# The modulation map of a diffusion step: from split matmuls through the weight ring to plain float32 on four column groups

## What is computed

```python
mod = (jax.nn.silu(cond) @ P['w_ada'][l] + P['b_ada'][l]).reshape(cond.shape[0], N_MOD, D_MODEL)
shift1, scale1, gate1, shift2, scale2, gate2 = (mod[:, i, None, :] for i in range(N_MOD))
h = rmsnorm(x, P['g_pre_mix'][l]) * (1 + scale1) + shift1
... = jnp.split(h @ P['w_in'][l], SPLIT_IDX, axis=-1)   # attention, mLSTM, conv, three gates
...
merged = (g[:, :, 0] * (merge_heads(att) @ P['w_br_na'][l])
          + g[:, :, 1] * (hm @ P['w_br_m'][l])
          + g[:, :, 2] * (hc @ P['w_br_cv'][l]))
x = x + gate1 * rmsnorm(merged @ P['w_out'][l], P['g_post_mix'][l])
h2 = rmsnorm(x, P['g_pre_ffn'][l]) * (1 + scale2) + shift2
ff = (jax.nn.silu(h2 @ P['w_ffn_gate'][l]) * (h2 @ P['w_ffn_up'][l])) @ P['w_ffn_down'][l]
x = x + gate2 * rmsnorm(ff, P['g_post_ffn'][l])
```

## Time and profile before

| | |
|---|---|
| median of 3 runs | 1340.09 us (1340.06 to 1340.61) |
| profiled execution, span from the first to the last instruction | 1337.3 us |
| PE busy | 1278.6 us, 96% |
| ACT busy | 446.9 us |
| DVE busy | 486.8 us |
| POOL busy | 504.7 us |
| data moved | 123.8 MB, mean 93 GB/s |

### The profile page before, as it was taken

How to read it: one execution, slowest core, us unless ns; L and a number is a source line. 1 busy time by engine, 2 the same in 40 slices (tenths; PEclk the granted TensorE clock), 3 DMA queues, 4 the chain that set the end, 5 groups by cost and what they waited for, 6 DMA issues and landing times. The chain is left out here.

```text
span 1337.3 us, 20142 instructions
## 1 busy us (share of the span) xinstructions
PE 1278.6 (96%) x8253; PEld 1186.7 (89%) x8253; DVE 486.8 (36%) x851; ACT 446.9 (33%) x757; POOL 504.7 (38%) x339
## 2 busy tenths in 40 slices
PE   5899999998999999999999989899999999999997
PEld 4699899998999889999999967789999999988886
DVE  5624444438444544454263372520000000041413
ACT  6524343332223333232334334632221222142431
POOL 3330330122222323564467546733333333324332
PEclk8799999998999999999999989899999999999999
DMA  8894472447525234665486526432222222212201
GB/s 289 174 120 61 64 79 35 51 61 79 55 59 62 63 80 78 97 86 105 110 160 166 133 81 192 136 88 70 79 78 77 64 78 79 74 53 81 92 32 79
DMA packets 166117, 123.80 MB, mean 93 GB/s; under 512 B 10079, under 2 KB 152535, under 8 KB 166039
## 3 DMA queue, kind: packets, MB, share of 16 engines
q1 hardware_dynamic: 163639, 118.23, 42.8%
q0 software_dynamic: 2400, 4.46, 1.1%
HBM read 119.00 MB, written 3.67 MB: 92 GB/s over the span
## 5 line engine op out<-in xcount | busy, mean ns | idle before, releaser
L599 POOL TENSOR_TENSOR w_lo<-raw,w_hi 128x1024 fp32r<-128x1024 f32 x166 | 409.3, 2478 | 603.1 <-ACT w_hi L875 602.9
L1579 PE MATMUL ps<-h_hi,w_hi 128*128 128x320 f32 x1744 | 547.5, 314 | 7.3 <-DVE h_lo L1553 2.3
L1581 PE MATMUL ps<-h_hi,w_lo 128*128 128x320 f32 x1744 | 540.3, 310 | 0.0
L1580 PE MATMUL ps<-h_lo,w_hi 128*128 128x320 f32 x1744 | 540.2, 310 | 0.0
L1579 PEld LDWEIGHTS ps<-h_hi,w_hi 128*128 128x128 f32 x1744 | 328.7, 188 | 11.9 <-issue 4.9
L1580 PEld LDWEIGHTS ps<-h_lo,w_hi 128*128 128x128 f32 x1744 | 328.8, 189 | 0.0
L1581 PEld LDWEIGHTS ps<-h_hi,w_lo 128*128 128x128 f32 x1744 | 328.6, 188 | 0.0
L875 ACT ACTIVATE w_hi<-raw 128x1024 fp32r<-128x1024 f32 x206 | 212.7, 1050 | 207.4 <-PE ps L1581 183.5
L1579 PE MATMUL ps<-w_hi,h_hi 128*128 128x512 f32 x300 | 118.8, 396 | 6.3 <-POOL w_lo L599 6.3
L1253 DVE TENSOR_TENSOR ff<-ps,sg 128x320 f32 (+1 forms) x44 | 21.6, 492 | 279.1 <-PE ps L1581 279.1
L1580 PE MATMUL ps<-w_lo,h_hi 128*128 128x512 f32 x300 | 118.0, 393 | 0.0
(11 more groups left out here) (223 smaller groups left out, 1302.2 us busy)
## 6 DMA issues: line engine op xcount, KB each, us to landing
raw<-in_w_in SPq DMA_DIRECT2D x64, 512.0 KB, 9.2
raw<-in_w_ada SPq DMA_DIRECT2D x48, 512.0 KB, 4.8
raw<-in_w_ffn_gate SPq DMA_DIRECT2D x22, 512.0 KB, 3.8
raw<-in_w_ffn_up SPq DMA_DIRECT2D x22, 512.0 KB, 3.8
raw<-in_w_ffn_down SPq DMA_DIRECT2D x22, 512.0 KB, 3.8
raw<-in_w_out SPq DMA_DIRECT2D x16, 512.0 KB, 3.9
xt<-in_x_sample SPq DMA_DIRECT2D x4, 512.0 KB, 8.2
raw<-in_w_br_cv SPq DMA_DIRECT2D x4, 512.0 KB, 3.4
```

The source lines that it names most:

```text
L599: ins = ve.tensor_tensor(w_lo[:, s, :], raw[:, s, :], w_hi[:, s, :].bitcast(F32), ALU.subtract)
L1579: nc.tensor.matmul(dst, wh, xh, start=first, stop=False)
L1580: nc.tensor.matmul(dst, wh, xl, start=False, stop=False)
L1581: return nc.tensor.matmul(dst, wl, xh, start=False, stop=last)
```

## The change

**The weights.** The modulation map leaves the ring. SP loads whole rows of `w_ada`: chunk k of vector m is 128 rows of 4 KB, one transfer of 512 KB (`load_ada`, two chunks at a time, numbered u = 0 to 23). The sixteen transfers for m = 1, 0 go to memory of their own: `ada1` lies over the ring's `w_hi` and `w_lo`, so ACT's first four splits wait for the vector m = 1, and `ada0` lies at the end of the memory. The other vectors share a double buffer `adaw`. The two `ada_81`, `ada_82` in the rows below are `ada1` and `ada0`.

**The products.** They are plain float32, not split. `cond` is 128 x 32 for each chunk, two columns of it used and the others zero. One step `("ada", idx, kp)` is four matmuls of 512 columns for two chunks and two halves of the vector; the four write to four groups of 32 partitions of one PSUM bank, so that each uses 32 columns of the array (`ada_bank`). Vector number idx takes four steps, in the order `ADA`. ACT (or for the gates DVE, with bias and gain, L1340, L1341) copies the bank to `adarow`, now 128 x 512. `ada_fold` (L1771) sums the groups and turns the row to columns with eight matmuls for the whole vector. `ada_wide` (L1780) brings a quarter of a gate to all partitions with one matmul of 512 columns, and DVE copies it (L1351).

**The start.** The order of SP is: x, seven pairs of the map's chunks, the ring's first two blocks, the eighth pair, the ring's next two. On PE all transposes of x come first, then the map, then unit ("q", 0). Its four groups are run with the chunks outermost, in four banks at once. The scale and shift of x (`h`) are shared: even chunks on DVE, odd ones on POOL.

**The late vectors.** `late_ada` spreads the steps over 56 slots, one for each group of the units `gate` and `br` of branches 0 and 1 (from the second quarter of branch 0 on). A load has a slot of its own one behind the step that frees its buffer. The last four slots, at the groups of `br` (1, 3), hold the four `ada_wide` of m = 5. The output projection now waits for all gates (`ada_wrd`).

Smaller parts: POOL loads the bias and gain of the gates with twelve transfers (`bb`); the fill of `mv` with ones on POOL moves behind the start; the constants shrink by 248 columns.

```diff
+ADA = (1, 0, 4, 3, 2, 5)
+
+
+def late_ada():
+
+    late = [[("ada_load", 8), ("ada_load", 9)], []]
+    for idx in range(2, len(ADA)):
+        for kp in range(KD // 2):
+            u = 4 * idx + kp
+            last = kp == KD // 2 - 1
+            late.append([("ada", idx, kp)] + [("ada_row", idx)] * last)
+            late.append([("ada_load", u + 2)] if u + 2 < 24 else [])
+            if last and ADA[idx] in (4, 3):
+                late.append([("ada_fold", idx)])
+            elif last:
+                late += [[("ada_wide", idx, q)] for q in range(4)]
+            else:
+                late.append([])
+    return late
...
     def unit(n):
+        if n == 0:
+            use(0, 0, 1)
+            plan.append(("unit0",))
...
+            if late and UNITS[n][0] in ("gate", "br") and UNITS[n][1] >= (0, 1) and UNITS[n][1][0] < 2:
+                plan.extend(late.pop(0))
...
+    plan.append(("xnorm",))
+    for k in range(KD):
+        plan.append(("xturn", k))
+    for kp in range(KD // 2):
+        plan.append(("ada", 0, kp))
+    plan.append(("ada_row", 0))
+    plan.append(("ada", 1, 0))
+    plan.append(("ada_fold", 0))
+    for kp in range(1, KD // 2):
+        plan.append(("ada", 1, kp))
     split_to(2)
...
+    plan += [("ada_row", 1), ("ada_fold", 1)]
+    for i in range(KD // 2):
+        plan += [("h", i), ("hsplit", i)]
...
+            def load_ada(u):
+                idx, kp = divmod(u, KD // 2)
+                for i in range(2):
+                    sp.dma_start(ada_tile(u)[:, i, :], ada_source(ADA[idx], 2 * kp + i)).then_inc(ada_in[u if u < 8 else 8 + u % 2], 16)
+
...
+            for u in range(7):
+                load_ada(u)
+            load(0)
+            load(1)
+            load_ada(7)
             load(2)
...
+                    if u == 8:
+                        sp.wait_ge(bo_lod, 8)
+                    elif u == 9:
+                        sp.wait_ge(hm_tr, TT)
+                    else:
+                        sp.wait_ge(ada_mm, u - 1)
+                    load_ada(u)
                 elif step[0] == "ml" and step[1] == 1 and ML_UNITS[step[2]][0] == CH:
...
+                    act.wait_ge(ada_mm, 4)
                 if b >= BLOCKS_HELD:
...
+                elif step[0] == "ada_wide":
+                    _, idx, q = step
+                    j = idx - 4
+                    w = 4 * j + q
+                    dve.wait_ge(ada_wd, w + 1)
+                    if w == 4:
+                        for s in c_out:
+                            dve.wait_ge(s, 64)
+                    half_, c = divmod(q, 2)
+                    nc.vector.tensor_copy((g1, g2)[j][:, c, half_ * 512:half_ * 512 + 512], A[w % 2]).then_inc(ada_wrd, 1)
+                elif step[0] == "out_start":
+                    dve.wait_ge(ada_wrd, 8)
...
+                elif step[0] == "ada":
+                    _, idx, kp = step
+                    u = 4 * idx + kp
+                    if u < 8:
+                        pe.wait_ge(ada_in[u], 32)
+                    else:
+                        pe.wait_ge(ada_in[8 + u % 2], 32 * ((u - 8) // 2 + 1))
+                    if u == 0:
+                        pe.wait_ge(cond_rd, 1)
+                    if u == 8:
+                        pe.wait_ge(hm_out, TT)
+                    if kp == 0 and idx in (3, 4):
+                        pe.wait_ge(ada_rd, idx)
+                    if kp == 0 and idx == 5:
+                        pe.wait_ge(ada_sum, 1)
+                    for i in range(2):
+                        for half_ in range(2):
+                            q = 32 * (2 * i + half_)
+                            ins = nc.tensor.matmul(ps[q:q + 32, ada_bank(idx), :], cond[:, 2 * kp + i, :],
+                                                   ada_tile(u)[:, i, half_ * 512:half_ * 512 + 512],
+                                                   start=(kp == 0), stop=(kp == KD // 2 - 1))
+                    ins.then_inc(ada_mm, 1)
+                elif step[0] == "ada_fold":
+                    idx = step[1]
+                    pe.wait_ge(ada_rd, idx + 1)
+                    dst = fold_of(idx)
+                    for k in range(KD):
+                        half_, o = divmod(k * P, 512)
+                        ins = nc.tensor.matmul(dst[:, 2 * k:2 * k + 2], adarow[:, o:o + P], sel[:, 2 * half_:2 * half_ + 2],
+                                               start=True, stop=True)
+                    ins.then_inc(ada_fd, 1)
+                elif step[0] == "ada_wide":
+                    _, idx, q = step
+                    w = 4 * (idx - 4) + q
+                    pe.wait_ge(ada_sum, idx - 3)
+                    if w >= 2:
+                        pe.wait_ge(ada_wrd, w - 1)
+                    nc.tensor.matmul(A[w % 2], sel[:, q:q + 1].to_broadcast([P, P]), adarow[:, :],
+                                     start=True, stop=True).then_inc(ada_wd, 1)
+                elif step[0] == "unit0":
+                    mine = [g for g, x in enumerate(GROUPS) if x["unit"] == 0]
+                    for g in mine:
+                        bank_free(g)
+                    for k in range(KD):
+                        pe.wait_ge(h_lod, k + 1)
+                        for g in mine:
+                            f, h = GROUPS[g]["what"]
+                            ins = three(ps[:, GROUPS[g]["bank"], 0:HT], weight(w_hi, 0, k, f), weight(w_lo, 0, k, f),
+                                        h_hi[:, k, half(h)], h_lo[:, k, half(h)], k == 0, k == KD - 1)
+                            if k == KD - 1:
+                                ins.then_inc(gemm_done, 1)
```

More of the change, by code:

```diff
@@ L67, in weight_units @@
     u = []
-    ada = lambda which, i: ("ada", (which, i), KD, UW)
-    for i in range(4):
-        u += [ada(1, i), ada(0, i)]
     for p in range(2):
@@ L78, in weight_units @@
         u += [("cc", p, KD, UW), ("cx", p, KD, UW), ("cb", p, KD, UW)]
-    late = {2: [[(4, i)] for i in range(4)], 0: [[(3, i)] for i in range(4)],
-            1: [[(2, i), (5, i)] for i in range(4)]}
     for b in (2, 0, 1):
@@ L85, in weight_units @@
             u.append(("gate", (b, i), KD, UW))
-            extra = [ada(*x) for x in late[b][i]]
-            u += extra[:1]
             u.append(("br", (b, i), 4, UW))
-            u += extra[1:]
     for r in range(2):
@@ L191, in make_plan @@
     side = []
+    late = late_ada()
     def unit(n):
+        if n == 0:
+            use(0, 0, 1)
+            plan.append(("unit0",))
         for j, emit in enumerate(tiles(n)):
-            if j % 2 == 0 and j // 2 < parts_of(n):
+            if n and j % 2 == 0 and j // 2 < parts_of(n):
                 use(n, j // 2)
@@ L268, in make_plan @@
         n += 1
-    while pending:
-        group("ada_col", pending.pop(0))
+    assert not late
     plan += [("out_split", 6, 8), ("out_start",)]
@@ L379, in release_of @@
     by_column = block_shape(b) == (KD, P)
-    mine = [g for g, x in enumerate(GROUPS) if x["unit"] == n and x["kind"] not in ("ada_col", "vt", "mvt", "kout")
+    mine = [g for g, x in enumerate(GROUPS) if x["unit"] == n and x["kind"] not in ("vt", "mvt", "kout")
             and (not by_column or x["what"][0] == p)]
@@ L518, in program @@
         vc_in, br0_in, br_in, state_in = sems("vc_in br0_in br_in state_in")
-        bc1_in, bc2_in = sems("bc1_in bc2_in")
+        bb_in, bb_zero = sems("bb_in bb_zero")
+        ada_in = [sem(f"ada_in{i}") for i in range(10)]
+        ada_mm, ada_rd, ada_sum, ada_fd, ada_wd, ada_wrd = sems("ada_mm ada_rd ada_sum ada_fd ada_wd ada_wrd")
         xb_in = sems("xb_in0 xb_in1")
@@ L606, in weight @@
                 return block_of(buf, BLOCK_OF[n, 0])[:, k, f * P:(f + 1) * P]
[L607 removed]
+            if kind in ("out", "down"):
                 per = block_shape(BLOCK_OF[n, 0])[0]
@@ L617, in source @@
             k0, c0 = 0, 0
-            if kind == "ada":
-                m, k0, c0 = "w_ada", 4 * part, which[0] * D + which[1] * UW
-            elif kind == "br":
+            if kind == "br":
                 m, c0 = ("w_br_na", "w_br_m", "w_br_cv")[which[0]], which[1] * UW
@@ L1039, in _ @@
                     drain(step[1])
+                elif step[0] == "ada_row" and ADA[step[1]] not in (2, 5):
+                    idx = step[1]
+                    act.wait_ge(ada_mm, 4 * idx + 4)
+                    if idx:
+                        act.wait_ge(ada_fd, idx)
+                    nc.scalar.activation(adarow[:, :], ps[:, ada_bank(idx), :], ACT.Copy).then_inc(ada_rd, 1)
                 elif step[0] == "hsplit":
                     for k in (2 * step[1], 2 * step[1] + 1):
-                        act.wait_ge(h_aff, k + 1)
+                        act.wait_ge(h_aff_pool if k % 2 else h_aff, k // 2 + 1)
                         nc.scalar.activation(h_hi[:, k, :], xnt[:, k, :], ACT.Copy).then_inc(h_hid, 1)
@@ L1594, in group @@
                     bank_free(g, rnd)
[L1595 to L1612 removed]
+                if kind == "vt":
```

(11 more changed lines are left out.)

220 lines of the change are left out of this document (97 added, 123 removed).

## The result

The changed kernel takes 1343.99 us (median of 20 runs, 1340.44 to 1346.62) against 1339.95 us before (20 runs): a ratio of 1.003, 95% interval 1.0023 to 1.0038. It is slower by 0.3%, where 1.3% faster was forecast (1322), and it lies outside the range of 1313 to 1338.

What follows compares the result with a forecast made beforehand. PE was taken as the bound, busy 1278.6 of 1337.3 us. Savings of 8.6 (late map), 3.4 (end of merge stage) and 6.0 (start) make 18 us: span 1319.3, plus 2.8 to the median, 1322; range 1313 to 1338.

Steps and rivals of the forecast that it cites:

- costed at nothing: the late loads: Merge stage: a 1 MB pair takes 2.5 us at 422 GB/s within 5.3 us of slots, about 20 us ahead; no cost.
- the failure of this cover: Merge stage: if the late loads' lead of about 20 us fails, each of eight waits costs one or two us.
- A late step: Merge stage: four matmuls in side-by-side column groups take 0.33 + 0.86 + 0.25 = 1.44 us; sixteen take 23.0.
- a fold: Merge stage: eight matmuls, sixteen records, summing the groups and turning the row take 1.95 us; two take 3.9.
- a broadcast: Merge stage: one matmul of 512 columns takes 0.86 + 0.25 = 1.1 us; four before br (1, 3) take 4.4.
- the term 0.33: Within a late map step: all other column groups are under way 0.33 us after the first, read from L1725.
- the stretch up to br (1, 3): Late part of the map before that unit: 31.3 us against 39.9, so 8.6 us less.
- The end of the merge stage: From br (1, 3) to the output projection: 16.9 us against 20.3, so 3.4 less (0.8 if the wait stays).
- PE's wait at the third broadcast: In br (1, 3): PE waits 3.7 us for DVE's copy behind the six splits, at most the 6.3 of before.
- The start: Kernel start: last pair in at 39, first unit begins at 48.5 and ends at 65.0 instead of 71.0, 6.0 us less.
- The two on the column groups: Late steps: groups run in sequence, 3.7 us a step, 1366 (chance 0.07); or records block the queue, 2.4, 1337 to 1339 (0.14).
- the signs of being wrong: A step over 2.5 us, PE waiting for late loads of `adaw`, or the projection's second unit waiting for its blocks.

Runs made afterwards that it cites:

- e1: Changed kernel with only the first late pair (u = 8) issued one unit earlier on SP: 1333.7 us, ratio 0.996.
- e5: Changed kernel with all late pairs issued earlier, later ones in the slot of the step freeing their buffer, bias and gain at slot 20: 1322.0 us.
- e9: As e5, but with POOL's twelve transfers of bias and gain at slot 0 again, as in the changed kernel: 1317.4 us, ratio 0.9843.
- e4: Changed kernel with first late pair early, bias and gain later, and 14 of 16 late pairs never loaded (not the layer): 1315.2 us.

## Why the prediction was wrong

**The step that failed** is "costed at nothing: the late loads". It set a pair at 2.5 us of transfer in 5.3 us of slots, and gave it the lead of the ring's loads, about 20 us, because it stands in the same queue. Both halves were wrong. In their place stood three waits, in steps of 17.4, 7.3 and 2.2 us where an unhindered step takes 1.09. With the low clock behind them they cost 26.5 us.

*The lead.* The 2.5 us are a rate and say nothing about when a load is issued. A ring load stands far ahead of its use, at the split of a block four places older. The first `ada_load` stands two slots ahead of its step, the others five or more. SP runs in order and cannot reach that place before it has issued the ring load in front, and this waits for POOL's split. The split in turn waits for a place in `w_hi` and `w_lo`, which is free only when PE has left an old block. Around 645 us the chain is this: PE goes on to the next block at 644.15, ACT splits from 644.77, POOL until 648.26, SP issues the ring load at 648.29 and the map's pair at 648.71. So SP comes by some 4 us after PE has changed blocks, and a load of the map has only its own distance in the plan as a lead. The three that were late had been issued 2.8, 9.2 and 13.7 us before PE wanted them.

*The transfer.* 422 GB/s was read from the start, where rows of 4 KB had the engines to themselves. Late, the same rows shared them with ring blocks of 512-byte rows and with POOL's transfers, and in the first wait the engines moved 148 to 272 GB/s at full share. A transfer of 512 KB landed after 8.4 us in the median and 17.5 at most. A lead of 13.7 us would have been ample for 2.5 us, and was not for this. The runs show the lead as the larger part (e1, e5, e9); how much the slow transfers would cost with a lead of 20 us was not measured, but in e9, with leads of at least 10 us, it is 1.4 us.

The prediction had a price for the failure of this cover, one or two us for each of eight waits. That sum, 8 to 16 us, would have given 1330 to 1338, which is still too low: it had more waits than came, and the two that counted were far longer.

**A late step** was taken at 1.44 us and takes 1.09; a fold 1.95 and 1.70; a broadcast 1.11 and 0.86 (0.46 until the next matmul starts and 0.40 until its successor does). The mechanism was right, the term 0.33 for the late start of the other groups was not. (In the kernel before the second half of L1725 does start 0.28 us late, at 130.61; the four groups of a step start together. What makes the difference was not tested.) Without the waits the stretch up to br (1, 3) would have gained more than forecast: in e4 the unit begins at 754.98, 18.3 us earlier than before, of which 4.4 are the start's, so some 14 where 8.6 were forecast.

**The end of the merge stage** came out as forecast. It took 17.2 us from 779.95 to 797.19, 16.9 were forecast, and PE's wait at the third broadcast was 3.84 us, released by L1351, where 3.7 were forecast. It answers to the 5.98 us of the earlier trace rows. The six splits took 6.17 us instead of the 9.53 of the earlier trace rows, beside one split of POOL, and ended 8.5 us into the unit, where 8.7 were set. Two terms were off and made up for each other, which is luck: the broadcasts took 1.0 us less, and the low clock 1.1 more.

**The start.** The last pair was there at 40.4 (39 forecast), scale and shift at 46.8 (45.3), the unit began at 50.07 (48.5) and ended at about 66.2 (65.0), 4.8 us earlier than before, not 6.0. The fold of sixteen records at the low clock took 3.58 where 3.0 were set.

**Rivals.** The two on the column groups had a chance of 0.21 together and were the wrong worry. What came true, PE waiting for late loads of `adaw`, stood among the signs of being wrong, with no chance of its own.

## What to carry to other kernels

A load in an in-order queue is issued when the entries ahead of it let it pass, not when its buffer is free. For each load that is added, look up the entry in front of it, what that waits for, and how far ahead of the use it comes; here the places of the late loads in the list decided some 25 us. Compare this lead with a landing time read where the queue is busy, not with bytes divided by a rate that was read where one kind of transfer ran alone.

## What the runs showed of the hardware

Four plain float32 matmuls of 512 columns into four groups of 32 columns take 1.09 us in all, into one group 3.64, measured between the plain matmuls around them: 3.3 times as fast. The Trainium skill ("TensorE: Matmul & The Clock Gate", "Part 3: Packing small matmuls — row/col tiling") measures 2.38 times for three narrow column tiles, and these traces agree with it in kind. The rule that the prediction had drawn from the same section, that tiles on the same rows run one by one, does not hold here; the section's own sentence speaks of loading weights, and not of the matmuls. Transfers with rows of 4 KB that were alone ran at 413 GB/s at full share (10 to 20 us), beside 512-byte rows and POOL's twelve transfers at 148 to 272 (595 to 610 us, above):

```profile
10.00:20.00 10.00, 4.69 (x22) 4.69 (x23) 4.51 (x7) 3.45 (x8) 3.83 (x7) 1.00 1.03 413
```
